# A hybrid Fourier / RWKV-7 layer with a mixture of experts: the products that nobody reads are taken out of the scan

## The reference

```python
def wkv7_scan(r, w, k, v, kk, a, s0, reverse):
    def step(S, inp):
        r_t, w_t, k_t, v_t, kk_t, a_t = inp
        sa = jnp.einsum('bhij,bhj->bhi', S, -kk_t)
        S = (S * w_t[:, :, None, :] + sa[..., None] * (kk_t * a_t)[:, :, None, :]
             + v_t[..., None] * k_t[:, :, None, :])
        y = jnp.einsum('bhij,bhj->bhi', S, r_t)
        return S, y
...
def parallel_mixer(...):
    proj = h @ w_in
    o_f = fourier_mix(u_f) @ w_fo
    y_f, bonus_f, s_f = rwkv7_direction(..., s_f0, False)
    y_b, bonus_b, s_b = rwkv7_direction(..., s_b0, True)
    ...
    return merged @ w_out, s_f, s_b
...
def trunk_layer(...):
    mix, s_f, s_b = parallel_mixer(h, ...)
    x = layer_norm(DEEPNORM_ALPHA * x + g1 * mix, ln1_g, ln1_b)
    h2 = x * (1.0 + sc2) + sh2
    x = layer_norm(DEEPNORM_ALPHA * x + g2 * expert_choice_ffn(h2, ...), ln2_g, ln2_b)
```

## Time and profile before

| what | us |
|---|---|
| median of 3 runs | 2633.46 (2632.03 to 2636.31) |
| profiled execution, its own time | 2636.95 |
| span of the profiled execution, first to last instruction | 2635.1 |
| PE busy in the span | 2426.6 (92%) |
| DVE, ACT, POOL busy | 1012.2, 636.7, 359.1 |

### The profile page before, as it was taken

How to read it: one execution, slowest core, us unless ns; L and a number is a source line. 1 busy time by engine, 2 the same in 40 slices (tenths; PEclk the granted TensorE clock), 3 DMA queues, 4 the chain that set the end, 5 groups by cost and what they waited for, 6 DMA issues and landing times. The chain is left out here.

```text
span 2635.1 us, 58505 instructions
## 1 busy us (share of the span) xinstructions
PE 2426.6 (92%) x26407; PEld 1546.8 (59%) x26407; DVE 1012.2 (38%) x1770; ACT 636.7 (24%) x1207; POOL 359.1 (14%) x402
## 2 busy tenths in 40 slices
PE   6999997698999989989799769999999999999997
PEld 4999995587787777778696423333333333333333
DVE  3344311658477576574345611212121212121214
ACT  2121222435445345343320101111111111111111
POOL 0000000315325134144002400000000000000000
PEclk8999998799999999999999879999999999999998
DMA  9363331010000000000092199999999999999984
GB/s 347 131 221 102 114 114 61 20 44 5 27 25 5 27 26 5 27 8 4 19 332 66 56 369 392 404 385 404 384 405 387 401 385 405 383 405 384 404 328 160
DMA packets 181023, 538.29 MB, mean 204 GB/s; under 512 B 13382, under 2 KB 54054, under 8 KB 180648
## 3 DMA queue, kind: packets, MB, share of 16 engines
q1 hardware_dynamic: 177704, 524.34, 52.2%
q0 software_dynamic: 2976, 10.16, 1.8%
q10 hardware_dynamic: 96, 0.05, 0.0%
HBM read 504.15 MB, written 30.38 MB: 203 GB/s over the span
## 5 line engine op out<-in xcount | busy, mean ns | idle before, releaser
L1818 PE MATMUL ps_h_lat<-w_piece,xT 128*64 128x512 f32 x2048 | 456.8, 599 | 10.7 <-DVE hidden L1944 7.5
L1818 PEld LDWEIGHTS ps_h_lat<-w_piece,xT 128*64 128x64 f32 x2048 | 146.0, 138 | 314.9 <-issue 314.9
L1938 DVE TENSOR_TENSOR hidden<-sigmoid_lat,ps_h_lat 64x1024 f32<-64x1024 f32 x32 | 39.1, 1223 | 506.5 <-ACT sigmoid_ctx L1711 506.5
L1843 PE MATMUL ps_y_lat<-w_piece,hiddenT 128*64 128x512 f32 x1024 | 232.6, 596 | 0.0
L1827 PE MATMUL ps_h_ctx<-w_piece,xT 128*16 128x512 f32 x2048 | 226.1, 593 | 0.0
L325 PE MATMUL ps_in<-hT_hi,w_in_hi 128*128 128x320 f32 x752 | 174.3, 313 | 2.6 <-issue 2.6
L672 POOL TENSOR_TENSOR Mo<-x,levels_sb 128x256 f32<-128x256 f32 x200 | 162.2, 834 | 99.2 <-PE ps_scan L914 99.1
L325 PE MATMUL ps_in<-hT_lo,w_in_hi 128*128 128x320 f32 x752 | 172.3, 310 | 0.0
L325 PE MATMUL ps_in<-hT_hi,w_in_lo 128*128 128x320 f32 x752 | 172.1, 310 | 0.0
L914 PE MATMUL ps_scan<-TT_diag,Mo 64*64 64x64 f32 x3200 | 117.3, 223 | 43.5 <-issue 27.2
L1843 PEld LDWEIGHTS ps_y_lat<-w_piece,hiddenT 128*64 128x64 f32 x1024 | 70.0, 137 | 137.7 <-issue 137.1
(11 more groups left out here) (310 smaller groups left out, 3580.2 us busy)
## 6 DMA issues: line engine op xcount, KB each, us to landing
w_piece<-in_w_e SPq DMA_DIRECT2D x192, 2048.0 KB, 15.8
w_ada<-in_w_ada SPq DMA_DIRECT2D x12, 2048.0 KB, 15.3
w_in_raw<-in_w_in SPq DMA_DIRECT2D x23, 1024.0 KB, 6.4
rkv_scratch<-projected SPq DMA_DIRECT2D x24, 320.0 KB, 6.4
rkv_T<-rkv_scratch SPq DMA_DIRECT2D x8, 960.0 KB, 5.4
gates_scratch<-projected SPq DMA_DIRECT2D x16, 320.0 KB, 6.8
gate_sb<-gates_scratch SPq DMA_DIRECT2D x8, 640.0 KB, 6.5
x<-in_x_sample SPq DMA_DIRECT2D x8, 512.0 KB, 12.3
```

Source lines behind the costliest of these rows:

```text
L1818: last = pe.matmul(psA[rows, cs], x[:, k, A], w[:, q, cs], start=(k == 0), stop=(k == KD - 1))
L1843: last = pe.matmul(psY[rows, :], hT[:, f, A], w[:, q, c * 512:(c + 1) * 512], start=(hf == 0 and f == 0), stop=(hf == 1 and f == FK - 1))
L1938: v.tensor_tensor(hid[A, :], sg[UP, :], psA[UP, :], ALU.mult)
```

## The change

`fill` returns at once, and the 161 products are gone. No other instruction is added or moved, and no wait.

```diff
             def fill(n):
 
-                for _ in range(n):
-                    pe.matmul(F[0][:, TOK:1024], causal[:, 0, 0, :], causal[:, 0, :, :], start=True, stop=True)
+                return
 
             def turn(n, i, m, last):
```

## The result

The changed kernel takes 2639.27 us (median of 12 runs, 2628.91 to 2646.39), and the kernel before, in the same runs, 2632.59 us (12 runs, 2630.65 to 2636.31). The ratio is 1.0017, with a 95% interval of 1.0009 to 1.0025: slower, by 2.4 to 6.6 us. The two medians lie 6.7 us apart; the means of the two sets of twelve lie 4.9 apart, since the changed kernel's executions scatter over 17.5 us and those of before over 5.7. I had forecast 2631, on the other side of no change. The profiled execution took 2639.31 us (mean granted clock 0.958), against 2636.95 (0.966) for that of before.

A forecast was written before the change was run, and what follows sets the result against it. PE's order of work, the longest string in the scan, was taken as the bound. Removing fillers wins 12.6 us, four clock falls cost 10, leaving 2.6 us less: forecast 2631 us, range 2620 to 2642.

The forecast's parts named there:

- The order's gain: PE's order of work without the fillers: 1.47 us less a full tile, 12.6 us less in all.
- in the last round: Before group 1, ACT's four copies start earlier without the two fillers: 0.42 us won a tile.
- in chunks 1 and 2 together: Two fillers between X and U in each chunk, partly hidden by ACT's `Xs`: 0.4 us won.
- at U of `CT`: Two fillers between X and U of `CT` and 0 lie on the path: 0.33 us won in full.
- ahead of chunk 3: Two fillers behind `output(m, 1)`, ahead of X of chunk 3: gain between 0 and 0.32 us, taken as 0.32.
- The price of a fall: Time lost to one fall to half clock in a chain: 2.5 us, between 1.7 and 3.4.
- The number of falls: Clock falls expected in the chains: 4, from two places in eight tiles at two falls in eight.
- two such places: Thin stretches opened in each tile: last round with the chain's head, and chunk 1 to 2; four falls expected.
- the comparison of 1.63 with 1.53 us: PE busy time per 3.40 us: 1.63 left at the chain's head without fillers, 0.1 above a stretch that fell.
- The first, no fall: Rival: the clock never falls in the chains, so the full 12.6 us are won, 2621 us; chance 0.28.
- The second, "falls nearly everywhere": Rival: clock falls in nearly every chain, from the last round to U of chunk 0: 2641 us, chance 0.2.
- The third, everything hidden: Rival: all fillers lie in waits, so neither gain nor fall is seen: 2633 us, chance 0.08.

The follow-up runs named there:

- Keep in waits: Kernel before with only the nine fillers a tile that lie in PE's waits kept (72 of 161): 2620.32 us, ratio 0.9945.
- two places: Kernel before with only six fillers a tile kept, three behind the last round and three behind S of chunk 1 (48): 2620.67 us, ratio 0.9949.
- first places dropped: Kernel before without the nine fillers a tile in the last round, behind it and ahead of U of `CT` (89 left): 2633.16 us, ratio 1.0002.
- drop in waits: Kernel before without the nine fillers a tile that lie in PE's waits (89 left): 2647.96 us, ratio 1.0055; further traces 2643.50 and 2637.12 us.
- Short fillers: Kernel before with all 161 fillers in place, but 16 columns each for 384: 2642.06 us, ratio 1.0029.
- the kernels with padding: Ten fillers ahead of `pair_products` in seven tiles, added to the changed kernel (2643.61 us) and to the kernel keeping only the 72 fillers in waits (2633.74 us).

## Why the prediction was wrong

**The order's gain was right.** Forecast 1.47 us a full tile, measured 1.53. Two of its terms were off, and by luck in opposite directions: in the last round 0.61 for 0.42, in chunks 1 and 2 together 0.28 for 0.4. The others came as forecast: at U of `CT` 0.32 for 0.33, ahead of chunk 3 0.32 for 0.32. Over the eight chains it is 280.4 - (7 * 33.62 + 31.72) = 13.3 us for 12.6. "Keep in waits" and "two places" confirm it at the end: both are 13 us below the kernel before beside them. The waits forecast (0.66 and 0.7 us) came as 0.69 and 0.59.

**The price of a fall was right in the mean.** Forecast 2.5 us, in a range of 1.7 to 3.4. Over the four traces of the changed kernel the chains lose 17.9, 10.0, 14.3 and 17.9 us in 7, 3, 5 and 7 falls: 2.7 each. But the places differ, 1.6 us between the chunks and 2.9 to 4.6 at the head, and most falls at the head lie beyond my range: in eight of eleven the clock stayed down for 10.2 us, three of the stretches of 3.4 where I had allowed for two.

**The number of falls is the step that failed**: "I give each tile two such places more at the same rate: 2 * 8 * 2/8 = 4 falls". It was 22 in four executions, 5.5 each, 0.34 a place for 0.25. At my own price of 2.5 us the sign turns at five falls (12.5 us for 12.6 won), so this step alone decides it. Giving both places the same rate was right: each has 11 of the 22.

The rate was miscounted in the trace of before. Its stretches were compared in windows that do not lie alike on them. The 2.08 us at 752.4, which I took for a denser stretch that held, is the same thin stretch a little too early; 0.9 us later the window has 1.18, less than the 1.35 and 1.53 ahead of the falls in tiles 1 and 2, and the clock held. A third fall, at 1233.7, I left out:

```profile
506.60:510.00 3.40, 1.15 (x32) 1.04 (x32) 2.67 (x6) 1.21 (x4) 3.26 (x6) 1.00 0.00 0
753.30:756.70 3.40, 1.18 (x33) 1.04 (x32) 3.40 (x7) 1.22 (x2) 0.00 (x0) 1.00 0.00 0
...
1230.30:1233.70 3.40, 1.47 (x44) 1.23 (x40) 1.13 (x2) 0.22 (x1) 3.12 (x5) 1.00 0.00 0
1233.70:1237.10 3.40, 3.40 (x70) 3.40 (x68) 1.18 (x2) 0.16 (x1) 3.19 (x6) 0.50 0.02 5
```

So the busy share of such a stretch does not tell whether it falls, and the comparison of 1.63 with 1.53 us had no ground. The thin stretch stands in seven tiles and not in eight (the last tile has no next one, and its work differs), and 2 of 7 makes 4.6 falls. Taken with the two other stretches of the scan that are as thin (1.15 us of 3.40 at 506.6, 1.47 at 1230.3), behind which it fell both times, it is 4 of 9, or 7.1 falls and 17.8 us: slower. One trace allowed anything from a gain to a loss.

A rate counted at one place is not that of another either, nor of the same place in another kernel: "first places dropped" has this thin stretch fall in all seven tiles. And falls of neighbouring tiles may hang together. In the changed kernel a chain with one short fall makes the tile 102.3 to 102.4 us long, and the place fell again 102.4 us later in all three such cases (at 1096.2 and 1198.6 us in the first trace, at 787.5 in the last); where the tile was 102.9 to 103.1 long it did not, in three cases. That is suggestive and no more: 22 falls in 64 places give 6 pairs of neighbouring tiles with a fall at the same place, as many as independent falls would (6.6).

In sum: 13.3 us won and 15.0 lost in the chains, in the mean of the four traces, for 12.6 and 10 forecast. The check from the other side: "two places" without a fall takes 2620.7 us, and 15.0 more is 2635.7; the mean of the four profiled times is 2636.2. The median of the changed kernel lies 3 us above that, and where these 3 us come from stays open. One fall more in the untraced executions would make them, but their mean clock (0.955 to 0.963) does not tell it: the traced execution with three falls and one with seven both show 0.959.

**The rivals.** The first, no fall, did not come in any of the four traces. The second, "falls nearly everywhere", named 2641 us and the head; its time is nearest, but half of the falls lay at the other place. I gave it 0.2, and the counts above show that it should have had more. The third, everything hidden, is excluded by 33.6 for 35.1 us.

**Gaps ahead of a fall.** In the 3.4 us ahead of the falls in the changed kernel's chains no gap of PE is longer than 0.92 us (0.69 in the first seven tiles), and the clock fell; the rule on long idle gaps (the Trainium skill, "TensorE: Matmul & The Clock Gate", section "HAM oscillation") does not tell this case, and the measurement decides. The trace agrees with that page's section on a second failure mode, frequent small idles between groups of products: in the windows ahead of the two falls shown PE was busy 2.39 and 2.53 of 3.40 us.

**What stays open**: what sets the tile in which an execution's first fall comes. The same kernel fell in tiles 2, 3 and 8 once, and in tiles 3 to 8 another time.

## What to carry to other kernels

Products that nobody reads can be load-bearing for the clock: before they are taken out, find those that stand in waits, where they cost nothing and do the holding, and those on the path, which cost up to their full length (0.165 us here). Here three in each of the two longest waits (48 for 161) gave 0.5% less time than the kernel before; none at all gave 0.2% more, and the other set alone 0.6% more. And do not count on a fall rate read from one execution: count every thin stretch in it, take several traces, and look whether a fall comes back at the loop's own period.

## What was not expected of the hardware

Falls of the granted clock came at the same distance from tile to tile: 102.4 us in the changed kernel and in "first places dropped" (tiles of mostly 102.2 to 102.4 us), and 105.8 to 105.9 in the first further trace of "drop in waits", where the falls are at 874.1, 979.9 and 1085.8 us and lengthen their tiles to 106.2 (866.5, 972.7, 1078.9). "Short fillers" has 105.8 as well (667.8, 773.6, 879.4). So a fall may keep its own repetition going, by the length that it gives the tile; this is argued, since the kernels with padding, built to test it, decided nothing.

At half clock the loading of weights slows as the products do. The same eight loads for part U take 0.97 us in the second tile of the changed kernel, at full clock, and 1.83 us in the third, at half:

```profile
668.57 0.97 PEld L981 LDWEIGHTS ps_scan<-Xs,x 128*128 128x128 f32 x8
...
769.94 1.83 PEld L981 LDWEIGHTS ps_scan<-Xs,x 128*128 128x128 f32 x8
```
